# The level products of a chunked recurrence: 128x128 products made as 64x64 blocks on two halves of TensorE's columns

## The reference, cut to what matters

```
b = jnp.cumsum(gc, axis=2)                      # running log of the forget gates
decay = jnp.exp(b_t - b_s)   for s <= t         # per key channel k
att[t, s] = sum_k q[t, k] * decay[t, s, k] * k[s, k]
o = att @ v  +  (q * exp(b)) @ S
```

## Time and profile before

| | |
|---|---|
| median of 3 runs | 681.16 us (679.83 to 685.82) |
| span of the profiled execution | 678.3 us |
| PE busy | 648.7 us, 96% of the span |
| PEld busy | 549.5 us, 81% |
| DVE busy | 515.5 us, 76% |
| ACT busy | 350.8 us, 52% |
| POOL busy | 147.5 us, 22% |
| mean granted TensorE clock | 0.988 |

### The profile page before, as it was taken

The page is one execution under the profiler, slowest core; times in us unless marked ns, Lnnn a source line. Parts: engine busy times, 40 slices in busy tenths (PEclk is TensorE's granted clock), DMA queues, the critical chain, the costliest instruction groups (busy, mean ns, idle before and its releaser), DMA issues.

```text
span 678.3 us, 9631 instructions
## 1 busy us (share of the span) xinstructions
PE 648.7 (96%) x3812; PEld 549.5 (81%) x3812; DVE 515.5 (76%) x599; ACT 350.8 (52%) x350; POOL 147.5 (22%) x81
## 2 busy tenths in 40 slices
PE   8999999988999999999978999999999999999894
PEld 6999899988997897578866888888888888888651
DVE  4326446699767385668588999999999999999887
ACT  4538413322227151111505877777777777777733
POOL 0000514422130220300021011111111111100657
PEclk9999999999999999999789999999999999999998
DMA  8971111111612205059429999999999999998443
GB/s 284 380 286 63 63 63 63 63 63 63 188 61 65 79 17 197 1 169 411 172 68 363 372 372 413 415 413 400 418 406 408 408 405 416 406 409 348 132 166 132
DMA packets 48803, 163.10 MB, mean 240 GB/s; under 512 B 4279, under 2 KB 23435, under 8 KB 36477
## 3 DMA queue, kind: packets, MB, share of 16 engines
q1 hardware_dynamic: 41900, 137.15, 53.3%
q0 software_dynamic: 6864, 25.43, 9.9%
HBM read 142.61 MB, written 19.96 MB: 240 GB/s over the span
## 4 chain that ended last, share of the span: by engine, by line
PE 87%; DVE 8%; ACT 2%; POOL 1%; issue 1%; DMA 1%; SPq 0%; DVEq 0%
PE bank L1916 25%; PE bank L1928 13%; PE bank L1641 7%; PE bank L1642 7%; PE bank L1798 6%; PE bank L1634 5%; PE bank L1676 4%; PE bank L1906 2%; PE bank L2020 1%; PE bank L1833 1%; PE bank L1878 1%; PE bank L1938 1%; PE bank L1808 1%; PE bank L2032 1%; PE bank L1605 1%; PE bank L1606 1%
## 5 line engine op out<-in xcount | busy, mean ns | idle before, releaser
L1429 DVE TENSOR_TENSOR RA<-FA,RA 128x2048 fp32r<-128x2048 f32 x93 | 212.7, 2289 | 20.8 <-ACT RA L921 20.1
L921 ACT ACTIVATE RA<-FA 128x2048 fp32r<-128x2048 f32 x93 | 179.0, 1925 | 41.9 <-PE bank L1916 25.9
L1916 PE MATMUL bank<-RA 128*128 128x512 f32 x768 | 185.0, 396 | 2.8 <-DVE RA L1434 2.0
L1916 PEld LDWEIGHTS bank<-RA 128*128 128x128 f32 x768 | 141.1, 189 | 33.9 <-DVE RA L1434 2.4
L1641 PE MATMUL bank<-RA 128*128 128x272 f32 x432 | 109.1, 290 | 0.0
L1642 PE MATMUL bank<-RA 128*128 128x272 f32 x432 | 108.5, 288 | 0.0
L1928 PE MATMUL bank<-RA 128*128 128x512 f32 x384 | 89.9, 390 | 1.4 <-DVE RA L1439 1.4
L1928 PEld LDWEIGHTS bank<-RA 128*128 128x128 f32 x384 | 72.0, 188 | 16.5 <-DVE RA L1439 1.6
L1641 PEld LDWEIGHTS bank<-RA 128*128 128x128 f32 x432 | 81.6, 189 | 0.0
L1642 PEld LDWEIGHTS bank<-RA 128*128 128x128 f32 x432 | 81.5, 189 | 0.0
L1065 DVE TENSOR_TENSOR RA<-FA,RA 128x2048 fp32r<-128x2048 f32 (+1 forms) x18 | 48.6, 2699 | 26.7 <-ACT RA L770 26.3
(11 more groups left out here) (271 smaller groups left out, 813.6 us busy)
## 6 DMA issues: line engine op xcount, KB each, us to landing
FA<-w_up SPq DMA_DIRECT2D x32, 1024.0 KB, 7.3
FA<-w_gate SPq DMA_DIRECT2D x32, 1024.0 KB, 7.0
FA<-w_down SPq DMA_DIRECT2D x32, 1024.0 KB, 7.9
FA<-w_in SPq DMA_DIRECT2D x13, 1024.0 KB, 5.0
y_by_slot<-FA POOLq DMA_DIRECT2D x14, 512.0 KB, 7.8
y_by_slot<-FA POOLq DMA_DIRECT2D x1, 5120.0 KB, 21.2
FA<-w_out SPq DMA_DIRECT2D x4, 1024.0 KB, 5.0
FA<-x_prompt SPq DMA_DIRECT2D x8, 256.0 KB, 5.6
```

The source lines that it names most:

```text
L921: nc.scalar.activation(split[split_slot(bi, j)][0], raw[place], ACT.Copy).then_inc(m_hi, 1)
L1429: tt_(sl[1], raw[place], f(sl[0]), ALU.subtract).then_inc(m_lo, 1)
L1916: last = mm(out[:, :], xgT[par][x_][:, kt, :], w[w_][:, t, :], start=(kt == 0 and i == 0), stop=(kt == KT - 1 and i == 2))
```

## The change

In levels 1 to 6 each 128x128 product becomes two: the first 64 tokens of the chunk with themselves, into partitions 0 to 63 of the bank, and the last 64 with themselves, into partitions 64 to 127. The second's output partitions place it on the second half of the array's columns. In level 7 each product becomes one, the first 64 tokens as weights, the last 64 as stream, into the upper right quarter, on the first half of the columns. The other parts of the bank keep what they held; the masks don't take them. Level 0, the sample products, the waits, the banks and all other engines' programs are as before.

```diff
                     if p >= 3:
                         pe.wait_ge(s_pc, p - 2)
+                    to = bank[4 + p % 3]
                     for c in range(NC):
                         cols = slice(c * P, (c + 1) * P)
-                        last = mm(bank[4 + p % 3][:, cols], lf[:, h, cols], rf[:, h, cols], start=True, stop=True)
+                        first, second = slice(c * P, c * P + P // 2), slice(c * P + P // 2, (c + 1) * P)
+                        if li == 0:
+                            last = mm(to[:, cols], lf[:, h, cols], rf[:, h, cols], start=True, stop=True)
+                        elif li < LEVELS:
+                            mm(to[0:P // 2, first], lf[:, h, first], rf[:, h, first], start=True, stop=True)
+                            last = mm(to[P // 2:P, second], lf[:, h, second], rf[:, h, second], start=True, stop=True)
+                        else:
+                            last = mm(to[0:P // 2, second], lf[:, h, first], rf[:, h, second], start=True, stop=True)
                     last.then_inc(s_p, 1)
```

## The result

The changed kernel takes **677.6 us** (median of 15 runs, 673.3 to 681.5), the kernel before 682.4 us (15 runs taken with them, 679.2 to 685.8 but for one of 1080.3, which nothing on record explains): ratio **0.9925 [0.9904, 0.9946]**. That is within 1%, as forecast; the forecast of 674.7 us lies 2.9 us under the median and the range holds it. The profiled execution took 675.0 us, span 673.2 us (before: 678.3), mean granted clock 0.982 (before: 0.988).

The account below looks back on a forecast made before the run. TensorE (PE) was taken as the bound, with 87% of the chain. Gains of 2.84 + 1.25 + 0.29 + 2.06 = 6.44 us cut the span from 678.3 to 671.9, making the median 674.7 us; range 673.0 to 683.5.

Parts of the forecast that it names:

- Side by side or in turns: Level products: whether column halves work simultaneously (pair 116 ns) or one after the other (232 ns); side by side chosen.
- Rivals 1, 2 and 4: Halves take turns (682.2 us, chance 0.34); overlap in part (678.4, 0.11); each change between halves drains (about 707, 0.09).
- rival 1: Levels 1 to 6: the halves take turns, 232 ns a pair; run +1.1 us, 682.2; chance 0.34.
- the 112/110/111.5 ns of one array: Today's f32 passes: load 112 ns, stream 110, both together 111.5, so a pass costs the longer, not the sum.
- Levels 1 to 3: Block products there: 1.42 us less each in levels 1 and 2, 1.25 in level 3.
- The price of the width: Changing array width around a level: entry into 64 columns 0.15 us, exit to 128 columns 0.2 us.
- Levels 6 and 7: Copy of head 0 ends 1.83 us after level start; 2.54 against 3.57 us, 1.03 less each, 2.06 together.
- Levels 4 and 5: Head 3 still follows DVE's chain, so only head 3's own gain is left: 0.29 us together.
- the likeliest case: Blocks side by side without a fall of the clock: 674.7 us, chance 0.31.
- rival 3: Side by side, but the clock falls after longer waits in levels 4 and 5: 676 to 678 us, chance 0.15.
- Today's stretch, 4.05 of 6.0 us busy, keeps clock 1.00: Old trace, 142.8 to 148.8 us: one of two stretches between which the new ones in levels 4 and 5 stand.
- The 2.9 us that the prediction put around the span: Median of timed runs, 681.16 us, less profiled span, 678.3; added to the forecast span of 671.9.

Follow-up runs that it names:

- the grouped halves: Changed kernel, but each head issues its four first-half blocks, then its four second-half blocks, instead of alternating: 681.7 us (one run; 683.4 before).
- the quarters: Changed kernel, but levels 1 to 5 use four 32x32 blocks on the four column quarters: 677.3 us, ratio 0.9918 to the kernel before.
- the wait filled: Changed kernel plus 12 unused 512-column matmuls on PE ahead of head 3 in levels 4 and 5: 674.8 us, ratio 0.9886 to the kernel before.
- the last level alone: Kernel before, with only level 7 made as one 64x64 block a chunk, levels 1 to 6 whole products: 682.9 us (one run; 683.4 before).
- the split halves: The reordered copies, with level 5's copies also ahead of the first conv tile's steps: 671.6 us, ratio 0.9822 to the kernel before.
- the reordered copies: Changed kernel, but DVE's four copies for levels 4 and 5 go between the two conv tiles: 671.0 us, ratio 0.9827 to the kernel before.
- the quarters with the split: The split halves, but levels 1 to 5 use four 32x32 blocks on column quarters: 668.5 us, ratio 0.9796 to the kernel before.

## Why the prediction was right where it was, and wrong where it was not

- **Side by side or in turns: right.** The pass was put at 58 ns by interpolation; the trace has 58.3. The pair was put at 0.116 to 0.12 us and is 0.117. Rivals 1, 2 and 4 all named a dearer pair; the 7 ns between the halves' starts, with a pass every 58 ns on each, rule out all three, and the kernel with both blocks on one half shows what rival 1 would have looked like. The tiling rule of the Trainium skill ("TensorEngine Tiling (Array Packing)", Tiling Modes: tiles can load and multiply in parallel) agrees with the trace. The other one ("TensorE: Matmul & The Clock Gate", Part 3: a load overlaps a running matmul only when the row group differs) does not: both blocks use all 128 rows, and loads and matmuls of both halves run at once (starts at 94.87 and 94.88 us). The prediction was right to let the 112/110/111.5 ns of one array weigh against it, yet still gave turns 0.34.
- **Levels 1 to 3: right**, 1.43, 1.42, 1.33 for 1.42, 1.42, 1.25. The price of the width was set too high. At level 3, entering 64 columns cost 0.13 us: 0.21 us from the last projection matmul to the first pass (0.13 before), and 0.10 instead of 0.058 from the first pass to the second. Leaving cost 0.09: 0.15 us from the last pass to the next instruction, of which 0.058 is the pass itself. That is 0.22 together, where 0.35 was taken. Part was given back by head 3, which stands 0.08 us late for DVE's copy and has the slow first step of 0.10 again: 0.13 together, not 0.05.
- **Levels 6 and 7: right in mechanism, 0.35 us too small together.** The step that failed: that "DVE first evacuates another tile and starts the first copy 1.09 us after the level's start" was kept fixed. In the trace after, the evacuation ends and the copies begin 0.81 us after the start (176.08 against 175.27). In the trace before, the tile's last two instructions start at 178.66 and 179.01, 0.35 apart, so without a wait the copy would have started at 179.36, not at 179.55: the last 0.19 us were head 0's own matmuls, 0.9 us long then. The other 0.09 is the level's own later begin (the width). A number that two things set within 0.2 us of each other was held constant when one of them moved. The rows before first, then after:

```profile
178.66 0.44 DVE L1105 TENSOR_TENSOR FA<-FA,bank 128x272 f32<-128x272 f32 x1 [3.23 <-PE bank L1642]
179.01 0.43 DVE L1106 TENSOR_TENSOR FA<-FA,bank 128x272 f32<-128x272 f32 x1
```

```profile
175.38 0.44 DVE L1105 TENSOR_TENSOR FA<-FA,bank 128x272 f32<-128x272 f32 x1 [3.41 <-PE bank L1642]
175.73 0.43 DVE L1106 TENSOR_TENSOR FA<-FA,bank 128x272 f32<-128x272 f32 x1
176.08 2.60 DVE L1128 COPY_PREDICATED FA<-masks,bank 128x512 f32<-128x512 uint8 x4
```

- **Levels 4 and 5: wrong in the likeliest case, right in rival 3.** The wait came as worked out: head 3 at 4.70 us, idle 3.1 us for 3.2. The sum then took the stretches on either side of the new one in the earlier trace rows and chose no fall. Five profiled executions have such a wait, of 2.6 to 3.7 us (the changed kernel three times, the grouped halves, the quarters): all five lose the clock in level 4, three in level 5. It cost about 1.5 us where the fall was 3.4 us long (36.57 against 35.09 with the wait filled), and 4.0 us where the two falls made 10.2 us.
- **A step of the earlier trace rows that was not a bound at all.** "Today's stretch, 4.05 of 6.0 us busy, keeps clock 1.00" was true of one execution. The kernel with the last level alone and the one with old products in 4 and 5 have that very stretch, and lost the clock behind it, in three of their four levels 4 and 5. One profiled execution shows that a stretch can keep the clock, not that it does.
- **The total.** The forecast is the case without falls, and what comes nearest to it is the kernel with the wait filled, 674.8 us. The changed kernel's runs spread over 673.3 to 681.5 us; their median, 677.6, lies in rival 3's 676 to 678. The runs' clocks say the same. Of the changed kernel's 37 runs the middle one has a mean clock of 0.977, of the 55 runs of the kernel before whose clock is on record 0.981. Among the runs with 0.982, the changed kernel takes 675.0 to 676.6 us (8 runs), the kernel before 682.4 to 683.4 (7 runs): some 7 us apart at the same clock, where the medians of the first comparison are 4.8 apart. The mean counts falls anywhere in a run, and not all are the change's: between 318 and 365 us, behind it, the profiled executions have 10.2 us at 0.50 in seven cases of fourteen (the kernel before and all three of the changed kernel among them) and 13.7 to 20.5 in the others. So a single run's time can't be put down to levels 4 and 5 without its trace.
- **The span.** That 674.7 and the profiled execution's 675.0 agree so well is partly luck. The profiled span is 1.3 us over the forecast's 671.9: 1.2 from levels 4 and 5, 0.4 back from the other levels, 1.7 from the fall at 638.7 us (18.6 - 16.9), and so 1.2 us less elsewhere, of which 0.8 lies behind the last matmul (9.1 us to the end of the span, 9.9 before). The 2.9 us that the prediction put around the span were not all there: in nearly every run on record the time is 1.8 to 1.9 us over the span, so the profiled execution before took about 680.2 us, 1 us less than the median run. The fall at 638.7 is in the profiled executions of this kernel (all three times), of the quarters and of the split halves, and not in those with the wait filled, the reordered copies or the quarters with the split. It follows no wait that the change made (PE's waits ahead of it, 0.78 and 1.41 us, are the same before and after), and why it comes is open.
- **What the prediction left out.** The chance of a gain behind DVE's order was not seen: the same edit is worth 4.8 us behind the old order of DVE and, by the ratios, about 7.5 behind the new one. The Trainium skill says this in general ("TensorEngine Tiling (Array Packing)", PSUM Bottleneck: tiling speeds up TensorE, not the copies out of PSUM, which may then bound). The trace agrees: with halves, head 3 is late for a copy in all seven levels, by 0.1 us in levels 1 to 3 (at 1.53 us, heads 0.47 apart before it) and by 3.1 us of idle time in level 4.

## What to carry to other kernels

Small matmuls that shared no columns of the array ran side by side here, loads and all, when they alternated in the program; written one group after the other, they lost over a third of the gain (3.05 against 2.51 us, from 3.93). Before costing such an edit, follow what empties their banks: what PE gains turns into waiting for the copies, and a wait can cost the clock on top. The order of the engine that copies can then be worth about as much as the edit (0.6% and 0.75% alone, 1.7% together).

## What the runs showed that was not expected

- Idle time of 1.95 us ahead of dense work kept the clock in three of six places and lost it in three (the kernel before, the last level alone, the old products in 4 and 5). Waits of 1.7 us (both blocks on one half, twice) and 2.0 us (the reordered copies, level 5) kept it. A fall of 3.4 us cost about 1.5 us.
- A half of the array ran ahead of earlier work for the other half by about three passes (0.29 us), no more.
- On four quarters each quarter gives a pass of 32 columns every 32 ns, as a single one does, so passes start 8 ns apart on average (32 of them from 95.36 to 95.62 us with the split tile): four quarters work at once, at next to no cost to each other.
- GpSimd's exponents (line 621) and DVE's instructions beside them take longer when they overlap: a 128x16 copy on DVE took 1.90 us instead of 0.17 while one ran, a 128x1024 product 2.91 instead of 1.22, and GpSimd's own 3.94 instead of 1.90.
